# Last step of the output on VectorE and GpSimd together, half of a token block on GpSimd, the first block stored in two halves

## What is computed

```python
def rmsnorm(x, g):
    xf = x.astype(jnp.float32)
    xf = xf * lax.rsqrt(jnp.mean(xf * xf, axis=-1, keepdims=True) + RMS_EPS)
    return (xf * g.astype(jnp.float32)).astype(x.dtype)
...
    y = jnp.einsum('btd,de->bte', merged, w_out).astype(x.dtype)
    x_out = x + rmsnorm(y, g_post)
```

## Time and profile before

| | before |
|---|---|
| median of three runs | 2385.73 us |
| profiled execution | 2387.73 us |
| its span | 2386.1 us |
| TensorE busy | 2268.3 us (95%) |
| VectorE busy | 1471.4 us (62%) |
| ScalarE busy | 924.6 us (39%) |
| GpSimd busy | 246.6 us (10%) |
| last matmul of the projection ends | about 2364.4 us |
| first instruction of L2047 starts | 2369.60 us |
| last store issued | 2381.02 us |

### The profile page before, as it was taken

The page is one execution under the profiler, slowest core; times in us unless marked ns, Lnnn a source line. Parts: engine busy times, 40 slices in busy tenths (PEclk is TensorE's granted clock), DMA queues, the critical chain, the costliest instruction groups (busy, mean ns, idle before and its releaser), DMA issues.

```text
span 2386.1 us, 40435 instructions
## 1 busy us (share of the span) xinstructions
PE 2268.3 (95%) x16616; PEld 2228.7 (93%) x16616; DVE 1471.4 (62%) x1636; ACT 924.6 (39%) x1232; POOL 246.6 (10%) x293
## 2 busy tenths in 40 slices
PE   3799999999999999999999999998999998799996
PEld 3799999999999999999999999997898988799996
DVE  5867677766666666766666666664665667353233
ACT  4334334334433344444444444444553332122221
POOL 3100000000200000111000000001443112000000
PEclk8899999999999999999999999999999999899998
DMA  5243534354444444444444444447556564545322
GB/s 150 59 115 109 149 87 137 97 151 112 118 133 118 113 126 123 115 126 121 116 126 120 117 126 120 118 126 259 168 188 198 160 212 119 140 115 177 88 70 97
DMA packets 415437, 311.29 MB, mean 130 GB/s; under 512 B 11181, under 2 KB 376869, under 8 KB 413296
## 3 DMA queue, kind: packets, MB, share of 16 engines
q1 hardware_dynamic: 396432, 247.76, 37.8%
q0 software_dynamic: 18848, 61.25, 7.2%
HBM read 250.06 MB, written 58.90 MB: 129 GB/s over the span
## 4 chain that ended last, share of the span: by engine, by line
PE 86%; DVE 6%; DMA 3%; ACT 2%; POOL 1%; issue 1%; SPq 0%; DVEq 0%; ACTq 0%; POOLq 0%
PE pp L718 63%; PE pp L855 9%; PE pp L1036 8%; PE M L726 1%; PE M L910 1%; DMA gt_lo<-gated_scratch 1%; PE M L880 1%; DMA raw_b<-in_w_out_dram 1%; PE M L890 1%; PE M L956 1%; PE M L818 1%; DVE xa L1492 1%; DVE XA L1815 1%; POOL xt L2096 0%; DMA out_dram<-states 0%
## 5 line engine op out<-in xcount | busy, mean ns | idle before, releaser
L718 PE MATMUL pp<-xa,wa_hi 128*128 128x288 f32 x7680 | 1543.0, 296 | 26.9 <-DVE wa_lo L1449 15.2
L718 PEld LDWEIGHTS pp<-xa,wa_hi 128*128 128x128 f32 x7680 | 1234.7, 188 | 29.4 <-issue 10.9
L718 PE MATMUL pp<-xa,wa_lo 128*128 128x288 f32 x3840 | 1131.4, 295 | 0.0
L718 PEld LDWEIGHTS pp<-xa,wa_lo 128*128 128x128 f32 x3840 | 725.2, 189 | 0.0
L1449 DVE TENSOR_TENSOR wa_lo<-raw_a,wa_hi 128x1024 fp32r<-128x1024 f32 x274 | 340.8, 1246 | 253.3 <-ACT wa_hi L1074 253.2
L1074 ACT ACTIVATE wa_hi<-raw_a 128x1024 fp32r<-128x1024 f32 x274 | 289.1, 1056 | 225.1 <-PE pp L718 218.4
L1449 DVE TENSOR_TENSOR wa_lo<-raw_r,wa_hi 128x1024 fp32r<-128x1024 f32 x136 | 173.3, 1274 | 141.6 <-ACT wa_hi L1074 141.6
L1074 ACT ACTIVATE wa_hi<-raw_r 128x1024 fp32r<-128x1024 f32 x136 | 143.6, 1056 | 133.5 <-PE pp L718 133.5
L855 PE MATMUL pp<-gt_hi,wb_hi 128*128 128x288 f32 x768 | 171.9, 306 | 22.7 <-DMA gt_lo<-gated_scratch 22.7
L855 PE MATMUL pp<-gt_hi,wb_lo 128*128 128x288 f32 x768 | 167.0, 299 | 0.0
L855 PE MATMUL pp<-gt_lo,wb_hi 128*128 128x288 f32 x768 | 166.8, 299 | 0.0
(11 more groups left out here) (282 smaller groups left out, 2123.4 us busy)
## 6 DMA issues: line engine op xcount, KB each, us to landing
raw_a<-in_w_in_dram SPq DMA_DIRECT2D x206, 512.0 KB, 5.0
raw_r<-in_w_in_dram SPq DMA_DIRECT2D x68, 512.0 KB, 5.0
z_scratch<-zs POOLq DMA_DIRECT2D x60, 576.0 KB, 3.3
raw_b<-in_w_branch_dram SPq DMA_DIRECT2D x48, 512.0 KB, 4.3
raw_b<-in_w_out_dram SPq DMA_DIRECT2D x32, 512.0 KB, 4.2
gz<-z_scratch SPq DMA_DIRECT2D x48, 288.0 KB, 4.4
qkv<-z_scratch SPq DMA_DIRECT2D x24, 288.0 KB, 5.1
gt_hi<-gated_scratch SPq DMA_DIRECT2D x4, 1152.0 KB, 9.4
```

Of the source, the lines that this page charges most:

```text
L718: i = nc.tensor.matmul(out, ws[:, slot, k, :], xa[:, o, part, k, :], start=opens and k == 0 and s == 0, stop=k == HK - 1 and s == 2, skip_ ...
```

## The change

VectorE no longer takes block after block. It takes a list of pieces: the first block in two halves of 1024 channels, blocks 1 and 2 whole, the first half of block 3, and the sample block. GpSimd takes the second half of block 3, in two instructions, since it multiplies by `rs_y` first and adds `x_again` afterwards. SyncE stores each piece when it is ready: seven stores instead of five, the GpSimd half between the first half of block 3 and the sample block. The reciprocal now increments `ms_ready`, so that both engines can wait for it.

```diff
+HALVES = (slice(0, D // 2), slice(D // 2, D))
+Y_DVE = [(0, HALVES[0]), (0, HALVES[1]), (1, slice(0, D)), (2, slice(0, D)), (3, HALVES[0]), (NT, slice(0, D))]
+Y_POOL = [(3, HALVES[1])]
...
+            for n, (m, cols) in enumerate(Y_DVE):
+                sp.wait_ge(yout_ready, n + 1)
+                store_y(m, cols)
+                if n == len(Y_DVE) - 2:
+                    for k, (mp, cp) in enumerate(Y_POOL):
+                        sp.wait_ge(yout_pool, k + 1)
+                        store_y(mp, cp)
+            sp.wait_ge(y_stored, 16 * (len(Y_DVE) + len(Y_POOL)))
...
             dve.wait_ge(root_x_ready, NB + 1)
             dve.wait_ge(x_again_loaded, 32)
-            steps.link(nc.vector.reciprocal(rs_y, rs_y))
-            steps.end(1)
-            for m in range(NB):
+            nc.vector.reciprocal(rs_y, rs_y).then_inc(ms_ready, 1)
+            dve.wait_ge(ms_ready, NB + 2)
+            for m, cols in Y_DVE:
                 rows = P if m < NT else TS
-                nc.vector.scalar_tensor_tensor(y_tok[0:rows, m, :], y_tok[0:rows, m, :], rs_y[0:rows, m:m + 1],
-                                               x_again[0:rows, m, :], ALU.mult, ALU.add).then_inc(yout_ready, 1)
+                nc.vector.scalar_tensor_tensor(y_tok[0:rows, m, cols], y_tok[0:rows, m, cols], rs_y[0:rows, m:m + 1],
+                                               x_again[0:rows, m, cols], ALU.mult, ALU.add).then_inc(yout_ready, 1)
...
+            pool.wait_ge(x_again_loaded, 32)
+            pool.wait_ge(ms_ready, NB + 2)
+            for m, cols in Y_POOL:
+                nc.gpsimd.tensor_scalar(y_tok[:, m, cols], y_tok[:, m, cols], rs_y[:, m:m + 1], None, ALU.mult
+                                        ).then_inc(ypool_scaled, 1)
+            for n, (m, cols) in enumerate(Y_POOL):
+                pool.wait_ge(ypool_scaled, n + 1)
+                nc.gpsimd.tensor_tensor(y_tok[:, m, cols], y_tok[:, m, cols], x_again[:, m, cols], ALU.add
+                                        ).then_inc(yout_pool, 1)
```

More of the change, by code:

```diff
@@ L433, in hybrid_layer @@
         yout_ready, y_stored = sem("yout_ready"), sem("y_stored")
+        yout_pool, ypool_scaled = sem("yout_pool"), sem("ypool_scaled")
         block = ctx.enter_context(nc.Block())
@@ L700, in _, with store_y @@
                         out_weights(At(H_OUT + 2 * j + s, d, 4), d * (2 * P) + j * P, s)
-            for m in range(NB):
-                sp.wait_ge(yout_ready, m + 1)
+            def store_y(m, cols):
                 if m < NT:
-                    sp.dma_start(yp_v[:, m, :], y_tok[:, m, :]).then_inc(y_stored, 16)
+                    sp.dma_start(yp_v[:, m, cols], y_tok[:, m, cols]).then_inc(y_stored, 16)
                 else:
-                    sp.dma_start(y_sample[0, :, :], y_tok[0:TS, m, :]).then_inc(y_stored, 16)
-            sp.wait_ge(y_stored, 16 * NB)
+                    sp.dma_start(y_sample[0, :, cols], y_tok[0:TS, m, cols]).then_inc(y_stored, 16)
+            for n, (m, cols) in enumerate(Y_DVE):
[6 more added lines that the diff above has]
+            sp.wait_ge(y_stored, 16 * (len(Y_DVE) + len(Y_POOL)))
         @block.tensor
@@ L2037, in _ @@
             dve.wait_ge(ysq_done, KD)
-            steps.begin(0, 2)
+            steps.begin(0, 1)
             steps.link(nc.vector.tensor_reduce(ss_y, ysums[:, :, :], AXX, ALU.add))
             nc.vector.tensor_scalar(ss_y, ss_y, 1.0 / D, EPS, ALU.mult, ALU.add).then_inc(ms_ready, 1)
+            steps.end(1)
             dve.wait_ge(root_x_ready, NB + 1)
             dve.wait_ge(x_again_loaded, 32)
-            steps.link(nc.vector.reciprocal(rs_y, rs_y))
-            steps.end(1)
-            for m in range(NB):
+            nc.vector.reciprocal(rs_y, rs_y).then_inc(ms_ready, 1)
+            dve.wait_ge(ms_ready, NB + 2)
+            for m, cols in Y_DVE:
                 rows = P if m < NT else TS
-                nc.vector.scalar_tensor_tensor(y_tok[0:rows, m, :], y_tok[0:rows, m, :], rs_y[0:rows, m:m + 1],
-                                               x_again[0:rows, m, :], ALU.mult, ALU.add).then_inc(yout_ready, 1)
+                nc.vector.scalar_tensor_tensor(y_tok[0:rows, m, cols], y_tok[0:rows, m, cols], rs_y[0:rows, m:m + 1],
+                                               x_again[0:rows, m, cols], ALU.mult, ALU.add).then_inc(yout_ready, 1)
         @block.gpsimd
```

## The result

The changed kernel took 2390.02 us, the median of 20 runs (2388.09 to 2392.3); the kernel before, in the 20 runs shared with it, 2386.47 us (2384.92 to 2390.56). The ratio is 1.0014, with a 95% interval of 1.0007 to 1.002: slower by 1.7 to 4.8 us. A second series gave a ratio of 1.0015 (1.0006 to 1.0024). The forecast was 2388.5 us on a median of 2385.73, which is 2.8 us slower. Taken by itself, 2390.02 us lies at the very top of the stated range (2385.3 to 2390.0); 0.7 us of that is the base, since the kernel before had a median of 2386.47 in this series, and the difference of the medians, 3.55 us, would give 2389.3 on the base of the forecast.

The account below looks back on a forecast made before the run. TensorE bounds until 2364.4 us, then VectorE and the stores in a 16.5 us tail. Turns with GpSimd delay block 1's store, ending the span 2.85 us later; added to the 2385.73 median: 2388.5 us, range 2385.3 to 2390.0.

Parts of the forecast that it names:

- What bounds the tail: Final 16.5 us: VectorE sets when the store stream starts; then both run nearly level, DMA the later of the two.
- The two engines don't overlap: Changed tail: VectorE instructions with two SBUF inputs and GpSimd ones reading SBUF exclude each other; VectorE ends 2.0 us later.
- rival B: Changed tail: GpSimd doesn't block VectorE, the 1.14 us head start stays, 2384.6 us; chance 0.13.
- C: Changed tail: GpSimd gets no turn until VectorE has run through, last two stores late, 2388.2 us; chance 0.08.
- Who goes when: Changed tail: engines take turns; scaling (1.0 us) delays block 0's second half, addition (2.25 us) runs ahead of block 1.
- my upper bound of 2.25: GpSimd's scaling on 128x1024: at most 2.25 us, as much as with two inputs; 1.0 us was taken.
- the signs that were named: Changed tail: block 0's second half 2.1 us, block 1 4.5, GpSimd 2.2 and 3.0, DMA pause about 2376 to 2378.
- The part that gives: Tail: VectorE loses 1.13 us of work, first store issues 1.14 us earlier; alone, the end moves by 1.1 us.
- D: GpSimd's first instruction after rest or a new kind costs several us, or the program shifts: above 2390.5; chance with body shifts 0.07.

## Why the prediction was right, and where not

**What bounds the tail: right.** VectorE sets the start of the stream and DMA is the later one; without GpSimd's work VectorE needs a microsecond less and the tail stays at 16.5 us.

**The two engines don't overlap: right, and shown.** GpSimd idle or writing only: 10.46 us for VectorE's pieces. With both instructions: 13.40, forecast 13.4 (2383.0 - 2369.6). The scaling costs 0.86 us of VectorE (1.0 forecast), the addition 2.08 (2.25). Without GpSimd's work the tail is back at 16.5 us, so the two instructions are the cause of the whole 2.7 us. The instruction of the tail behaves like the others, so rival B falls, and so does C: the addition ended at 2375.33 us, 7.8 us into the tail.

**Who goes when: half right.** GpSimd and VectorE take turns. But I gave the scaling 1.0 us of time where it needs 2.85, from rows of selects and a memset; even my upper bound of 2.25 was too low. Blocked time and own time aren't the same for it. The addition therefore asked too late for the turn ahead of block 1 and took that ahead of block 2. The forecast had block 1's store at 2377.37, 7.8 us into the tail; it went out 5.6 us into it, and block 2's 10.0, as forecast (2379.6 is 10.0). That the end came out right in spite of this is in part luck: both turns fall ahead of block 2's end either way, so its store went out when forecast, and the forecast had put block 2's landing behind a late block 1 (2383.8, 14.2 us into the tail) where in fact it landed like a first store (2377.51 + 3.9, 13.9 us into it). All that follows was sized well, and the end moved by 2.7 us instead of 2.85: last landing 2380.96 + 5.4 = 2386.4 us, 18.8 us into the tail, forecast 2388.55, which is 18.95. The row for it:

```profile
out_dram<-y_tok SPq DMA_DIRECT2D x1, 512.0 KB, 5.4
```

Of the signs that were named, the second half of block 0 came (2.14 us for 2.1), and the tail started 5.2 us behind the last matmul (2362.37 us). Block 1 at 4.5 us did not: it took 2.34, and block 2 took 4.42. GpSimd's durations were 3.84 and 3.71 us, not 2.2 and 3.0, and the long pause of the DMA engines came 9.1 to 10.8 us into the tail, not 6.4 to 8.4.

**The part that gives: wrong.** "With nothing else, both limits move by 1.1 us, and the end with them" failed. Measured, they give 0.0 us (no work on GpSimd) and 0.1 (first block in halves). The numbers against it stood in the earlier trace rows: 3.9 us to landing for the first store, 4.4 for the third. A store in the middle waited only some 0.25 us for each one ahead of it, and by that reading a head start can't be worth more than the next store's wait. It didn't hurt the forecast because the sum had already given the head start up; it would have made rival B's 2384.6 us wrong by a microsecond, had B been true.

**D: not as priced.** Nothing cost several us more, and the body moves without a change of program. But the scaling did take 1.85 us more than I gave it, and its being the first of its kind is not excluded as the reason. These 1.85 us held up the addition, not VectorE.

**Slips in the sums.** 2385.73 + 2.85 is 2388.58, not 2388.5. The memset's 587 ns for 576 channels are 1.04 us for 1024 in proportion, not 0.97 (measured for that size: 0.95). In C, 2380.9 + 2.25 is 2383.15, not 2383.3. None of them changes the forecast by more than 0.1 us.

## What to carry to other kernels

Before work goes from VectorE to GpSimd, count what each instruction reads: if VectorE's have two inputs in SBUF and GpSimd's read SBUF, GpSimd's reading time is added to VectorE's: half a block, 1.2 us of work for VectorE, cost it 2.9 us when GpSimd took it. A stream of stores that is nearly level with its producer gained from an earlier start only when every later piece came earlier too (0.1 us with one block in halves, nothing with four, 0.7 with all five); look at how long each store waited in the queue before paying for a head start. And an effect of 3 us in 2386 is read from the stretch that changed, not from single runs whose bodies differ by 4 us.

## What the runs showed of the hardware that I had not expected

- GpSimd's scaling by a per-token factor on 128x1024 takes 2.85 us alone, more than the two-input addition (2.34 us), and shuts a two-input VectorE instruction out for 0.86 us only. Whether a second scaling would take as long no run shows. The Trainium skill ("SBUF — State Buffer", "Who interferes with whom") says that the winner holds the ports for the whole instruction; for the addition the runs agree (2.08 of 2.34 us), for the scaling they don't, if its recorded time is the instruction's.
- With both engines queued, the turn goes to the one that waits, instruction by instruction. The loss of 2.1 us fell on the VectorE instruction next to start when GpSimd's addition asked: on block 2 when it asked 4.1 us into the tail, on the second half of block 1 when it asked at the same moment but VectorE's blocks were halved, and on the second half of block 0 when it asked at 0.1 us.
- The store of 64 partitions (0.52 MB) holds the DMA engines for 2.7 us, in the middle of the stream as behind a pause, against the 2.2 us by which it landed behind block 3 before.
